# h by token behind the mLSTM, made from x by token and y at the first boundary

## What is computed

```python
h = concatenate([meta, x])                                   # 272 x 1024
h = h + 0.5 * rmsnorm(swiglu(rmsnorm(h, gn[0]), ...), gn[1]) # first FFN, "f0"
u = rmsnorm(h, gn[2])
y = mlstm_mixer(u, a_w_in, conv, gates, a_w_out)             # "a"
h = h + rmsnorm(y, gn[3])
h = h + 0.5 * rmsnorm(swiglu(rmsnorm(h, gn[4]), ...), gn[5]) # second FFN, "f1"
x = h[NMETA:]                                                # then two more layers, "l0", "l1"
```

## Time and profile before

| what | us |
|---|---|
| median of 3 runs | 784.53 (784.14 to 784.73) |
| profiled execution | 784.16 |
| its span | 782.0 |
| TensorE busy | 773.6 (99%) |
| VectorE busy | 579.5 (74%) |
| ScalarE busy | 415.2 (53%) |
| GpSimd busy | 117.5 (15%) |
| DMA, mean over the span | 207 GB/s |

### The profile page before, as it was taken

One profiled execution on the slowest core, in us unless ns is written; L12 is line 12 of the kernel. 1 busy time (PEld: TensorE's weight loads), 2 busy tenths in 40 slices (PEclk: granted clock), 3 DMA queues, 4 the chain that ended last, 5 costly groups with the idle time before them and its releaser, 6 DMA issues.

```text
span 782.0 us, 14582 instructions
## 1 busy us (share of the span) xinstructions
PE 773.6 (99%) x5764; PEld 731.0 (93%) x5764; DVE 579.5 (74%) x926; ACT 415.2 (53%) x731; POOL 117.5 (15%) x136
## 2 busy tenths in 40 slices
PE   9999999999999999999999999999999999999997
PEld 8999999999999999889999998889999988999985
DVE  6777767799696977588888888677676768567763
ACT  7544444445247566485445443556655557455541
POOL 3800000033230000000000000010054411035510
PEclk9999999999999999999999999999999999999999
DMA  9876667696416644478878786635474571754531
GB/s 348 302 263 245 217 236 241 217 330 204 159 55 220 209 155 141 129 260 311 291 276 289 267 289 213 229 135 188 143 237 135 163 269 40 237 182 136 156 114 54
DMA packets 46114, 161.93 MB, mean 207 GB/s; under 512 B 5168, under 2 KB 6736, under 8 KB 46048
## 3 DMA queue, kind: packets, MB, share of 16 engines
q1 hardware_dynamic: 46048, 161.01, 60.4%
HBM read 159.91 MB, written 1.08 MB: 206 GB/s over the span
## 4 chain that ended last, share of the span: by engine, by line
PE 89%; DVE 5%; ACT 2%; issue 2%; DMA 1%; SPq 0%; POOL 0%; DVEq 0%; POOLq 0%; ACTq 0%
PE ps L370 21%; PE ps L372 20%; PE ps L371 20%; PE ps L819 5%; PE ps L817 5%; PE ps L818 5%; PE ps L759 3%; DVE w L1233 2%; PE ps L674 1%; DVE cv L1537 1%; PE ps L618 1%; PE ps L749 1%; ACT w L870 1%; PE ps L730 1%; PE ps L739 1%
## 5 line engine op out<-in xcount | busy, mean ns | idle before, releaser
L1233 DVE TENSOR_TENSOR w<-raw,w 128x1024 fp32r<-128x1024 f32 x237 | 287.9, 1222 | 129.2 <-ACT w L870 128.9
L370 PE MATMUL ps<-u,w 128*128 128x256 f32 (+1 forms) x1275 | 364.7, 286 | 0.4 <-DVE w L1233 0.4
L372 PE MATMUL ps<-u,w 128*128 128x256 f32 (+1 forms) x1275 | 360.1, 282 | 0.0
L371 PE MATMUL ps<-u,w 128*128 128x256 f32 (+1 forms) x1275 | 359.8, 282 | 0.0
L870 ACT CAST w<-raw 128x1024 fp32r<-128x1024 f32 x237 | 246.1, 1049 | 114.8 <-PE ps L372 82.1
L370 PEld LDWEIGHTS ps<-u,w 128*128 128x128 f32 x1275 | 239.4, 188 | 5.4 <-issue 3.1
L372 PEld LDWEIGHTS ps<-u,w 128*128 128x128 f32 x1275 | 239.7, 188 | 0.0
L371 PEld LDWEIGHTS ps<-u,w 128*128 128x128 f32 x1275 | 239.5, 188 | 0.1
L1932 POOL TENSOR_SCALAR Sb<-Sb,st 128x256 f32<-128x256 f32 x32 | 45.1, 1426 | 95.1 <-DVE st L1701 95.1
L1251 DVE SCALAR_TENSOR_TENSOR acc<-adr,cact,acc 128x1024 f32<-128x1024 f32 x42 | 55.7, 1340 | 0.0
L914 ACT ACTIVATE si<-tmp 128x272 f32<-128x272 f32 (+1 forms) x40 | 17.0, 425 | 66.0 <-DVE tmp L1346 66.0
(11 more groups left out here) (269 smaller groups left out, 975.8 us busy)
## 6 DMA issues: line engine op xcount, KB each, us to landing
raw<-wst SPq DMA_DIRECT2D x245, 512.0 KB, 4.4
adr<-wada SPq DMA_DIRECT2D x48, 512.0 KB, 3.7
Bt<-bias_rows SPq DMA_DIRECT2D x8, 192.0 KB, 4.1
hT<-xT SPq DMA_DIRECT2D x4, 272.0 KB, 4.3
sq<-nrow SPq DMA_DIRECT2D x2, 512.0 KB, 4.7
g2row<-weight_rows SPq DMA_DIRECT2D x2, 512.0 KB, 5.8
sq<-weight_rows SPq DMA_DIRECT2D x2, 512.0 KB, 5.4
outT<-hT SPq DMA_DIRECT2D x4, 256.0 KB, 2.0
```

The source lines that it names most:

```text
L370: e.matmul(out, a, x1, start=first, stop=False)
L371: e.matmul(out, a, x2, start=False, stop=False)
L372: return e.matmul(out, b, x1, start=False, stop=last)
L1233: e.tensor_tensor(b, r, a.bitcast(F32), ALU.subtract).then_inc(*tick(s_split, k))
```

## The change

At the first boundary TensorE transposes the sixteen 128 x 128 tiles of yg (unscaled y times gain, tokens 16 to 271) into PSUM, eight in place of the six zero products behind the first spread and eight behind the second spread; `head` keeps two zero products in place of six. ScalarE copies them with the first scale to a new buffer ht (by token), two halves ahead of u1(0) and two ahead of u1(3). VectorE's `scaled(k)` waits until tile k is transposed, since it overwrites it. SP loads x by token (a new input, 2 x 512 KB) into xt, behind the loads of chunks 75 and 79. GpSimd adds xt to ht, four adds of 128 x 512, behind its memsets. xt lies over y1, so ScalarE's first write of y1 waits for the adds. `rows_of_h` is gone, and VectorE's `rows` reads h from ht. The squares of h wait for `rows` by another semaphore.

```diff
@@ head
-            def head(keys, c, x1, x2, n, high, low, fill=6):
+            def head(keys, c, x1, x2, n, high, low, fill=2):
-                dense(fill)
+                dense(fill, b_[0])
@@ tensor
+            def rows_of_y(hf):
+                for t in range(2):
+                    place(("yrow", t, hf), (4 + 3 * t) if hf else (rot[0] + 2 + t) % 4)
+                for j in range(4):
+                    k = 4 * hf + j
+                    e.wait_ge(*read(("out", "f0", k)))
+                    for t in range(2):
+                        m = e.transpose(ps[:, bank_of(("yrow", t, hf)), 128 * j:128 * j + 128],
+                                        yg[:, k, 16 + 128 * t:144 + 128 * t], ident)
+                    m.then_inc(*tick(s_yrow, k))
@@ both_scales
                 spread(("r1", s), 6, n, rst)
-                dense(6)
+                rows_of_y(0)
                 e.wait_ge(s_pow.handle, at(s_pow, ("r2", s)))
                 spread(("r2", s), 5, n, rst2)
+                rows_of_y(1)
@@ token_outputs
-                    if s == "a" and i in (n - 3, n - 2):
-                        rows_of_h(i - n + 3)
@@ scalar
+            def rows_of_y(hf):
+                e.wait_ge(s_pow.handle, at(s_pow, ("r1", "f0")))
+                e.wait_ge(s_yrow.handle, at(s_yrow, 4 * hf + 3))
+                for t in range(2):
+                    e.mul(half_row(htf, t, hf), ps[:, bank_of(("yrow", t, hf)), :], rst[:, t:t + 1]).then_inc(
+                        *reading(("yrow", t, hf)))
             def normalised(s, n):
+                rows_of_y(0)
                 for k in range(KT):
+                    if k == 3:
+                        rows_of_y(1)
@@ output on scalar
+                    if h == 0:
+                        e.wait_ge(s_xy.handle, at(s_xy, (1, 1)))
@@ vector
             def scaled(s, k, n):
+                e.wait_ge(s_yrow.handle, at(s_yrow, k))
@@ rows on vector
-                    e.scalar_tensor_tensor(h, h, rst[:, t:t + 1], ps[:, bank_of(("hrow", t, hf)), :], ALU.mult,
-                                           ALU.add).then_inc(*reading(("hrow", t, hf)))
+                    e.scalar_tensor_tensor(h, h, rst[:, t:t + 1], half_row(htf, t, hf), ALU.mult, ALU.add).then_inc(
+                        *tick(s_htok, (s, t, hf)))
@@ gpsimd
+            for t in range(2):
+                e.wait_ge(s_xt[t].handle, 16)
+                for hf in range(2):
+                    e.wait_ge(*read(("yrow", t, hf)))
+                    h = half_row(htf, t, hf)
+                    e.tensor_tensor(h, h, xt[:, t, 512 * hf:512 * hf + 512], ALU.add).then_inc(*tick(s_xy, (t, hf)))
@@ sync
+                if c + 1 in (76, 80):
+                    t = (c + 1 - 76) // 4
+                    e.wait_ge(s_proj.handle, at(s_proj, ("out", "f0", KT - 1)))
+                    e.dma_start(xt[:, t, :], xtok[128 * t:128 * t + 128, :]).then_inc(s_xt[t].handle, 16)
```

More of the change, by code:

```diff
@@ L100, with build @@
     dma_start = wait_ge = then_inc = same
-def build(nc, xT, wst, wada, vec, cst, tab, rb, nrow, outT):
+def build(nc, xT, wst, wada, vec, cst, tab, rb, nrow, xtok, outT):
     ctx = ExitStack()
@@ L162, in build @@
             if ax is None:
-                ax = ExitStack()
+                ax, xx = ExitStack(), ExitStack()
+                xt = sb("xt", [P, 2, D], F32, xx)
+                xx.close()
                 y1 = sb("y1", [P, NH, S], F32R, ax)
@@ L181, in build @@
                 den = sb("den", [P, 3, 4], F32, ax)
+                sb("line_end_a", [P, 20], F32, ax)
+                ht = sb("ht", [P, 2, D], F32, ax)
                 ax.close()
@@ L233, in flat @@
             return x[:, :, :].rearrange("p k t -> p (k t)")
-        ygf, hTf, vrow, tmf = flat(yg), flat(hT), flat(pair), flat(tmp)
+        ygf, hTf, vrow, tmf, htf = flat(yg), flat(hT), flat(pair), flat(tmp), flat(ht)
         GATED = 4
@@ L309, in build @@
         s_num, s_ytr, s_ptr, s_val = signal("numerators_done"), signal("y_transposed"), signal("p_transposed"), signal("values_done")
-        s_hrow, s_utr = signal("h_rows_done"), signal("u_transposed")
+        s_yrow, s_utr = signal("y_rows_done"), signal("u_transposed")
+        s_xt, s_xy = [signal(f"x_rows_landed{t}") for t in range(2)], signal("y_added_to_x")
         s_hg, s_htok, s_gtok, s_gtr2, s_gcol = signal("h_weighed"), signal("h_by_token"), signal("gates_by_token"), signal("gates_back"), signal("gates_by_feature")
@@ L549, in rows_of_gains @@
                 e.transpose(ps[0:2 * KT, b, 0:P], GG[:, l, :], ident).then_inc(*tick(s_rowt, l))
[L551 to L558, removed]
             def h_to_features(t, hf):
-                e.wait_ge(*read(("hrow", t, hf)))
+                e.wait_ge(s_htok.handle, at(s_htok, ("a", t, hf)))
                 b = place(("uta", t, hf), bank_of(("tok", "a", t, hf)))
@@ L1122, in squares_of_h @@
                 for hf in range(2):
-                    e.wait_ge(*(read(("hrow", t, hf)) if s == "a" else (s_htok.handle, at(s_htok, (s, t, hf)))))
+                    e.wait_ge(s_htok.handle, at(s_htok, (s, t, hf)))
                     if t:
@@ L1622, in rows @@
                     e.wait_ge(*read(("tok", s, t, hf)))
-                    e.wait_ge(s_hrow.handle, at(s_hrow, (t, hf)))
+                    e.wait_ge(s_xy.handle, at(s_xy, (t, hf)))
                     h = half_row(ygf, t, hf)
-                    e.scalar_tensor_tensor(h, h, rst[:, t:t + 1], ps[:, bank_of(("hrow", t, hf)), :], ALU.mult,
-                                           ALU.add).then_inc(*reading(("hrow", t, hf)))
+                    e.scalar_tensor_tensor(h, h, rst[:, t:t + 1], half_row(htf, t, hf), ALU.mult, ALU.add).then_inc(
+                        *tick(s_htok, (s, t, hf)))
                 def second_sum(t):
@@ L2150 @@
     arrays = {"xT": xT, "wst": wst, "wada": wada, "vec": np.ascontiguousarray(vec), "cst": c, "tab": tab,
-              "rb": np.ascontiguousarray(A(rel_bias_2).T), "nrow": np.ascontiguousarray(A(norm_gains)[0, 3:6:2])}
+              "rb": np.ascontiguousarray(A(rel_bias_2).T), "nrow": np.ascontiguousarray(A(norm_gains)[0, 3:6:2]),
+              "xtok": np.ascontiguousarray(A(x)[0])}
     nc = bacc.Bacc("TRN2", target_bir_lowering=False, num_devices=1, dynamic_dma_scratch_size=2048)
```

## The result

| | before | changed |
|---|---|---|
| median of 21 runs, us | 784.66 (783.89 to 786.87) | 786.59 (783.99 to 790.74) |
| ratio, 95% interval | | 1.0025 (1.0016 to 1.0034) |
| profiled execution, us | 784.16 | 785.98 |
| its span, us | 782.0 | 784.2 |
| TensorE waits named with over 1 us, after the start | none | 1.7 and 1.7 |

The kernel became 0.25% slower, 1.9 us.

What follows compares the result with a forecast made beforehand. VectorE was taken to be level with TensorE from 227.7 to 281.3 us, without slack. The terms -1.75 + 0.05 + 1.8 + 0.8 = +0.9 us on the median of 784.53 gave 785.4 us, range 782.5 to 787.0.

Steps and rivals of the forecast that it cites:

- slower: Whole kernel: a measured time from 786.1 us on; chance 0.24.
- What bounds the kernel: From 227.7 to 281.3 us: vector side level with TensorE, without slack; what VectorE loses before 243.5 us reaches the end.
- Part 1: Out projection behind the mLSTM: the sixteen transposes of h leave TensorE's chain, gaining 1.75 us.
- Part 2: First boundary: transposes of y replace zero products and ScalarE's reads stay hidden; cost 0 to 0.1 us, taken as 0.05.
- Part 3: SP's queue behind loads 75 and 79: two x loads of 512 KB by DMA, no cost in bandwidth.
- Part 4: Four GpSimd adds of 128x512 hold VectorE's instructions with two SBUF operands; cost 1.8 plus 0.8 us.
- the first pair: GpSimd's adds from near 232.5 us, among VectorE's splits and taps: 2 x 1.1 - 0.4 = 1.8 us lost.
- the second pair: GpSimd's adds after the x load landing near 244.6 us, around the last gate step: 0.8 us taken, up to 1.7.
- (c): VectorE at 243 to 246 us: both pairs of adds meet the gate chain, cost 3.9, 786.7 us; chance 0.17.
- (b): Only the first two adds cost, the others land behind the last gate step: 784.6 us; chance 0.58 together with the forecast.
- (a): Adds fit between VectorE's instructions or in its idle time, cost nothing on the chain: 782.8 us; chance 0.18.
- (d): TensorE from 210 to 216.4 us: transposes in place of zero products lower the clock, price 1.6 us, 787.0 us; chance 0.07.

Runs made afterwards that it cites:

- where h is transposed too: Changed kernel with all adds waiting for the last gate step and the sixteen transposes of h put back into the out projection: 784.23 us, ratio 0.9997 to before.
- the early kernel: Changed kernel with the second x load two chunks earlier on SP, behind load 77 in place of 79: 785.65 us, ratio 1.0023 to before.
- the seven other variants: All follow-up kernels except the changed kernel itself and the one with its second x load two chunks earlier; medians from 782.24 to 788.63 us.
- The scalings: Changed kernel with GpSimd's four adds replaced by four scalings by 1.0 with one SBUF operand, so x is not added: 782.75 us, ratio 0.9977 to before.
- the fast variants: Changed kernel with adds cut to one column, all held until the last gate step, or replaced by scalings: 782.24, 782.40 and 782.75 us.

## Why the prediction was right, and where it was not

The forecast was 785.4 us with a range from 782.5 to 787.0; measured were 786.6, in the range but near its upper end. The forecast expected +0.11%, and +0.25% (0.16 to 0.34) came; whether that is past the 0.2% from which I counted "slower", with a chance of 0.24, the interval leaves open. Against the profiled execution the sum was 784.16 + 0.9 = 785.1: three traces of the changed kernel have 784.94, 784.98 and 785.19, the first has 785.98. Step by step:

- **What bounds the kernel.** Right, and it decided the case. VectorE's chain from 227.7 to 281.3 us has no slack. In each of the twelve traces besides that of before, the span is 782.0 us plus the time by which the split at 229 us starts late, plus the loss of the stretch, less the 1.75 of the transposes (not where h is transposed too), and this holds to 0.15 us: losses of 1.65, 2.68, 3.12, 3.78 and 6.05 us all reached the end one for one, and 0.01 us left nothing. Had I gone by TensorE's 99% alone, I would have forecast 782.8.
- **Part 1**, 1.75 us of transposes: right (1.8 measured alone).
- **Part 2**, the boundary, 0.05 us: right; 0.07 at the head's start, 0.01 behind it. ScalarE's four reads took 1.27 and 1.26 us for two, as priced, and stayed hidden.
- **Part 3**, the loads: right. The first landed at 232.85, expected near 232.3, the second at 244.49, expected near 244.6.
- **Part 4**, the adds. A length of 1.27 us and more for one that nobody holds (1.24 expected), a hold of 1.03 to 1.09 us where it meets a tap or a gate step (1.1 taken), the first pair 1.65 (1.8 taken; the 2.1 that a hold for an add's full length would give is further off). The step that failed is the second pair: I took 0.8 us, a mean between landing ahead of both gate steps and landing behind them. In the first profiled execution it landed ahead of both and cost 2.12, more than the 1.7 that I gave as its most, since the second add of a pair also gets its turn between L1507 and L1508; in three other executions it cost 1.03. A landing near 244.6 against a step at 244.8 should have been read as "one step is held for sure", that is 1.1 to 2.1.
- **The nearness of 785.1 to three traces** is in part luck: the second pair was 0.2 us too small, the first 0.15 too large, and 0.2 us outside the span that the change saved (last section) stood in no term.
- **Rivals.** (c), both pairs meet the gate chain, is what the first trace shows, with 3.78 us against the 3.9 of its price; its first half (no idle time for the first pair) did not come about. (b) was the state of none of the four traces. (a) is dead: it comes true only with the adds taken away or moved.
- **(d), the clock**, did not happen in any trace. Busy time by stretch of the changed kernel (us, PE, PEld, DVE, ACT, POOL, granted clock, DMA share, GB/s):

```profile
212.00:217.00 5.00, 4.62 (x36) 3.64 (x36) 3.97 (x14) 1.69 (x3) 2.73 (x4) 1.00 0.18 66
257.00:262.00 5.00, 3.32 (x27) 3.08 (x26) 4.37 (x8) 4.11 (x9) 0.00 (x0) 1.00 0.42 133
283.00:287.00 4.00, 2.33 (x20) 2.00 (x20) 3.12 (x13) 3.39 (x9) 0.00 (x0) 1.00 0.51 161
```

It is 1.00, the 2.4 GHz level, over the boundary, where TensorE did little but spreads and transposes from 213.2 to 216.6, and over both waits. By the Trainium skill, "TensorE: Matmul & The Clock Gate", section "Part 4: PE-mode transpose", a transpose does not count as busy time for the clock in the way that a product does; these 3.4 us of spreads and transposes, sixteen transposes among them, did not lower it here. The price of (d) was also read from the wrong place: over the first 6 us of the kernel before, where the zero products of the earlier trace rows ran slowly, the granted clock is 1.00 as well, so no row of these traces gives the price of a lower clock.

**What stays open.** The changed kernel was executed 35 times in all, and 11 of these took over 787 us. Without them its median would be 785.45 in place of 786.00. Six of the 11 have a mean granted clock of 0.994, the five others 0.997 to 0.999, so the clock is not the whole of it. A clock of 0.994 was seen in 7 of the 35, in 1 of 12 of the early kernel, and in none of the 69 executions of the seven other variants or the 77 of the kernel before that were made beside the variants. It goes with kernels in which both pairs of adds hold VectorE; but the kernel with three times the adds, built to provoke it, is one of these and did not show it, and its five executions are too few to exclude one in five.

One execution that is too long was traced: the one of the kernel with three times the adds, 790.26 us where its four others have 788.24 to 788.73. Its loss to the adds is the 6.05 us of its stretch, which the median needs too. But it was 0.23 us behind the kernel before at its split of 26 us, and 2.16 at the boundary's first spread, ahead of every instruction of the change. Kernel before, then this one:

```profile
25.80 3.49 DVE L1233 TENSOR_TENSOR w<-raw,w 128x1024 fp32r<-128x1024 f32 x3
26.00:200.00 174.00, 174.00 (x1390) 174.00 (x1390) 133.44 (x160) 80.85 (x119) 22.39 (x26) 1.00 0.70 243
```
```profile
26.03 3.49 DVE L1251 TENSOR_TENSOR w<-raw,w 128x1024 fp32r<-128x1024 f32 x3
26.00:200.00 174.00, 174.00 (x1376) 174.00 (x1375) 133.50 (x161) 80.89 (x118) 22.24 (x26) 1.00 0.69 242
215.17 0.59 PE L440 MATMUL ps<-cs,rst 128*128 128x128 f32 x3
```

From that split to the boundary's first spread the same work took 189.14 us in place of 187.21, with TensorE never idle, fewer of its instructions in the same time (1376 against 1390 in 174 us) and a granted clock of 1.00. So at least this rise has nothing to do with the adds; why TensorE was 1% slower, and whether the untraced long executions of the changed kernel are of this kind, is not shown. In the other traces the start of the split at 229 us is 0.04 to 0.89 us late, and it is so by the splits at 16 us already.

## What to carry to other kernels

An engine's idle time says little about the room beside it: GpSimd was 15% busy, and its adds cost 1.5 to 2.2 times what the change brought, because a GpSimd add with two SBUF operands held VectorE's instructions with two SBUF operands (1.03 to 1.09 us for a tap or a gate step), and VectorE was level with TensorE there. Before moving work to an idle engine, follow the chain of waits through the stretch where it will run, and look for rows in which the two engines' instructions already overlap. The same adds were free 12 us later, so a wait that holds background work back until the critical steps are through can be the whole repair.

## What the runs showed that I had not expected

- A gate step of eight partitions and 272 columns, 0.42 us long, waits just as long for an add as a full one: 1.51 us. The Trainium skill, "SBUF — State Buffer", section "Who interferes with whom", has an exclusive lock for the whole instruction of whoever issues first, between a VectorE instruction with two SBUF inputs and any GpSimd instruction that reads SBUF. The adds bear out that the two exclude each other and take turns, though VectorE lost 1.03 to 1.09 us for a meeting where an add by itself lasts 1.27. The scalings do not bear it out: one of 2.45 us with one SBUF operand left the split beside it at 1.23 us. VectorE's copies from PSUM kept their lengths beside an add; a VectorE instruction with one SBUF operand was not looked at.
- The time outside the span is shorter in the changed kernel and its variants: 1.74 to 1.94 us over all their executions, in the median 1.8, against 1.76 to 2.16 before, in the median 2.0. So some 0.2 us of the gain of the fast variants lies ahead of or behind all instructions. Nothing here says why.
